# Both products of a transformer MLP by seven products of halves, in two phases, on one Trainium2 core

## The reference, cut to what matters

```python
def sqrelu_mlp(xn, w1, w2):                   # xn (1024, 1024), w1 (1024, 4096), w2 (4096, 1024)
    return jnp.square(jax.nn.relu(xn @ w1)) @ w2

    f = sqrelu_mlp(rms_norm(h, g[2]), ffn_w1[i], ffn_w2[i])
    h = h + rms_norm(f, g[3])
```

## Time and profile before

| | |
|---|---|
| median of 3 runs | 2694.79 us (2693.78 to 2695.09) |
| the profiled execution's own time | 2696.62 us |
| its span, first to last instruction | 2694.4 us |
| mean granted TensorE clock | 0.977 |
| PE busy | 2523.3 us (94%), 12064 matmuls |
| DVE busy | 1754.1 us (65%) |
| POOL busy | 1235.9 us (46%) |
| ACT busy | 1037.8 us (39%) |
| MLP of layer 0, first projection to the end of `down_last` | from 955.9 us |
| MLP of layer 1, the same | from 2006.3 us |

### The profile page before, as it was taken

The page is one execution under the profiler, slowest core; times in us unless marked ns, Lnnn a source line. Parts: engine busy times, 40 slices in busy tenths (PEclk is TensorE's granted clock), DMA queues, the critical chain, the costliest instruction groups (busy, mean ns, idle before and its releaser), DMA issues.

```text
span 2694.4 us, 35810 instructions
## 1 busy us (share of the span) xinstructions
PE 2523.3 (94%) x12064; PEld 2078.4 (77%) x12064; DVE 1754.1 (65%) x3033; ACT 1037.8 (39%) x1849; POOL 1235.9 (46%) x661
## 2 busy tenths in 40 slices
PE   7899999798898999999999999977899999999998
PEld 6689877676676878888888887856777888888886
DVE  5599999766665566676566746175565765665565
ACT  5543533556555251223232235265543222223222
POOL 2112776544544123565566422366622465565541
PEclk9999989899999999999999999999999999999999
DMA  4471733533444621111221134654452121101213
GB/s 145 68 111 27 165 98 115 190 98 91 140 131 131 239 97 55 55 32 45 62 62 54 39 110 128 156 150 122 125 173 103 31 63 54 54 27 51 70 39 125
DMA packets 260043, 258.15 MB, mean 96 GB/s; under 512 B 11906, under 2 KB 219810, under 8 KB 257620
## 3 DMA queue, kind: packets, MB, share of 16 engines
q1 hardware_dynamic: 250436, 239.22, 31.6%
q10 hardware_dynamic: 9216, 16.78, 2.1%
q0 software_dynamic: 272, 0.62, 0.1%
HBM read 181.60 MB, written 74.97 MB: 95 GB/s over the span
## 4 chain that ended last, share of the span: by engine, by line
PE 78%; POOL 7%; DVE 6%; issue 4%; ACT 3%; DMA 1%; SPq 0%; DVEq 0%; POOLq 0%; ACTq 0%
PE ps L446 75%; POOL attn_out_split L1071 1%; POOL attn_out L1069 1%; PE ps L2318 1%; DVE probs_T L1930 1%; POOL w_split L398 1%; DVE logits L1895 1%; PE ps L564 1%; ACT relu_scores L1285 1%; DVE masks L1799 1%; POOL attn_out_split L1067 1%; DVE acc L1657 1%; POOL attn_out_low L1064 1%; ACT probs_T L1436 1%; DVE acc L1646 1%
## 5 line engine op out<-in xcount | busy, mean ns | idle before, releaser
L446 PE MATMUL ps<-xn_T,w_split 128*128 128x512 f32 x4608 | 1058.9, 391 | 1.6 <-DVE xn_T L1734 1.5
L446 PEld LDWEIGHTS ps<-xn_T,w_split 128*128 128x128 f32 x4608 | 867.6, 189 | 186.4 <-issue 3.0
L398 POOL TENSOR_TENSOR w_split<-w_raw,w_split 128x1024 fp32r<-128x1024 f32 x92 | 225.9, 2465 | 638.0 <-ACT w_split L391 637.7
L446 PE MATMUL ps<-w_comb,hid_comb 128*128 128x512 f32 x2016 | 458.9, 389 | 0.0
L446 PEld LDWEIGHTS ps<-w_comb,hid_comb 128*128 128x128 f32 x2016 | 378.4, 188 | 78.6
L2093 DVE TENSOR_TENSOR acc<-acc,ps 128x512 f32<-128x512 f32 x480 | 303.0, 683 | 77.7 <-PE ps L446 72.6
L446 PE MATMUL ps<-w_split,hidden 128*128 128x512 f32 x1344 | 310.8, 392 | 8.9 <-POOL w_split L398 6.3
L446 PEld LDWEIGHTS ps<-w_split,hidden 128*128 128x128 f32 x1344 | 253.5, 189 | 63.2 <-issue 6.6
L2073 DVE TENSOR_TENSOR hid_blocks<-hid_blocks 128x512 f32<-128x512 f32 x96 | 85.5, 891 | 263.9 <-ACT hid_blocks L1538 263.1
L594 POOL TENSOR_TENSOR w_split<-w_raw,w_split 128x1024 fp32r<-128x1024 f32 x52 | 132.8, 2555 | 247.7 <-ACT w_split L589 247.7
L1533 ACT ACTIVATE hid_comb<-hid_blocks 128x512 fp32r<-128x512 f32 (+1 forms) x120 | 95.2, 802 | 216.7 <-PE ps L446 84.4
(11 more groups left out here) (206 smaller groups left out, 3477.3 us busy)
## 6 DMA issues: line engine op xcount, KB each, us to landing
w_raw<-in_w SPq DMA_DIRECT2D x104, 512.0 KB, 4.2
q_scratch<-q_split SPq DMA_DIRECT2D x128, 128.0 KB, 2.5
q_tile<-q_scratch ACTq DMA_DIRECT2D x64, 256.0 KB, 2.7
cat_scratch<-attn_out_split SPq DMA_DIRECT2D x128, 128.0 KB, 2.6
w_raw<-in_w_in SPq DMA_DIRECT2D x30, 512.0 KB, 4.7
unit_tile<-cat_scratch SPq DMA_DIRECT2D x48, 256.0 KB, 3.6
h_scratch<-acc SPq DMA_DIRECT2D x24, 512.0 KB, 4.1
w_raw_rest<-in_w SPq DMA_DIRECT2D x24, 512.0 KB, 6.5
```

Source lines behind the costliest of these rows:

```text
L398: nc.gpsimd.tensor_tensor(whl[:, n0 % 4, 1, :], wraw[:, n0 % 4, :], whl[:, n0 % 4, 0, :].bitcast(F32), ALU.subtract).then_inc(w_lo, 1)
L446: return nc.tensor.matmul(out_ap, stat, mov, start=start, stop=stop)
```

## The change

In each layer the first 4 inner tiles are still computed directly by `project_first`. The other 28 go through "up" in seven products too, and the whole of "down" follows after the whole of "up":

- **Input sums.** The up product needs four sums of quarters of the input (`x_sums`). POOL forms three raw quarters (high plus low, `raw`: 6 operations of 128x1024, four of them while the normalisation still runs, two after the second transposes). DVE forms the fourth and the four sums (10 operations of 128x1024), and their low parts (8 of 128x1024); ACT their high parts.
- **First rows.** ACT does ReLU and square of the first 4 tiles. DVE brings them into the form of seven operands (8 sums of 128x512) between the input sums, before it takes out the first up product. Each layer then stores 14 such blocks (3.5 MB) to DRAM.
- **Up.** 7 iterations (LOOPS = 6 and one more) of two column pairs, 7 products each, a product is 12 matmuls into one PSUM bank: 14 x 12 = 168 matmuls an iteration. POOL: per pair 4 sums of w1 blocks and 7 low parts, all 128x512. DVE: per pair 8 operations from PSUM, 4 squares and 4 sums in SBUF, all 128x512. SP loads the next two w1 tiles and stores the pair's 7 blocks to a DRAM scratch (`h_operand_scratch`).
- **Down.** 28 products (4 groups of 7; the last group is half as deep). Per product: a load of its inner operand from the scratch (1 MB), high parts by ACT, low parts by DVE for the inner operand (`h_low`, 128x2048) and by POOL for w2 (`down_low`, 128x2048; 4 sums of the same size per group), 48 matmuls, takes by DVE as before. Then `change_quarters` once, and `down_last` for inner tiles 28 to 31.
- `sp_gains` of the MLP's end moves behind the up phase; `CREDIT` and the old rings go.

```diff
+        def half_pair(p, i):                      # POOL, per pair
+            k = 7 * p
+            a11, a12, a21, a22 = [w1_block(p, c, h) for c in range(2) for h in range(2)]
+            s2 = w1_operand(L, k + 2)
+            pool.wait_ge(w1_ld[p], loads + 32 + 32 * i)
+            nc.gpsimd.tensor_tensor(a21, a11, a21, ALU.subtract).then_inc(w1_sum, 1)
+            up_low(k, i)
+            up_low(k + 1, i)
+            pool.wait_ge(a_full, w1_slot_free(L, k + 2) + 14 * i)
+            up_sum(p, 1, i, s2, a22, a21, ALU.subtract)
+            up_sum(p, 2, i, a12, s2, a12, ALU.subtract)
+            nc.gpsimd.tensor_tensor(a11, s2, a11, ALU.add).then_inc(w1_sum, 1)
+            up_low(k + 2, i)
+            up_low(k + 3, i)
...
+        split_lo(pool, L["tf"] + LOOK)            # POOL, ahead of the loop
+        pool.wait_ge(a_full, first_pos(sn, 0, 0) + 1)
+        pool.wait_ge(a_free, trans_pos(sn, 0, KT - 1) + 1)
+        raw(0, 0, 0)
+        raw(1, 0, 4)
+        pool.wait_ge(a_free, trans_pos(sn, 1, KT - 1) + 1)
+        raw(3, 1, 4)
+        head(0)
+        with pool.Fori(0, LOOPS, 1) as i:
+            rest(i)
+            head(i + 1)
+        rest(LOOPS)
+        for g in range(4):                        # POOL, down
+            b11, b12, b21, b22 = [w_block(g, k)[:] for k in range(4)]
+            z = 7 * g
+            down_low(z)
+            pool.wait_ge(w2_ld[1], w_loads(lay, g))
+            pool.wait_ge(w2_ld[3], w_loads(lay, g))
+            down_sum(g, 0, b12, b22, b12, ALU.subtract)
+            down_sum(g, 1, b11, b12, b11, ALU.add)
+            down_low(z + 1)
+            down_low(z + 2)
+            down_sum(g, 2, b21, b11, b21, ALU.subtract)
+            down_low(z + 3)
+            down_sum(g, 3, b22, b22, b11, ALU.subtract)
+            for r in range(4, 7):
+                down_low(z + r)
...
         for j in range(4):                        # ACT
-            relu_square(first_pos(sn, j, 0), L["f0"] + j, j, 0)
-            square_hid(L["f0"] + j, j, 0)
+            relu(j, 0)
...
+        act.wait_ge(h_st, 128 * sn)
+        relu(0, 1)
+        relu(1, 1)
+        up_high(0, 0)
+        up_high(1, 0)
+        x_sum_high(6, 0)
+        x_sum_high(4, 2)
+        relu(2, 1)
+        x_sum_high(9, 3)
+        x_sum_high(11, 1)
+        up_high(2, 0)
+        up_high(3, 0)
+        relu(3, 1)
...
         xn_low(sn, 1, 0, KT)                      # DVE, ahead of the loop
+        for k in range(2):
+            js = slice(2 * k, 2 * k + 2)
+            raw12 = first_op(nc.vector.tensor_tensor(xsum[:, 2, js, :], xt[:, 1, 0, js, :].bitcast(F32), xt[:, 1, 1, js, :].bitcast(F32), ALU.add))
+        t3 = x_sum_op(2, 3, 2, ALU.subtract, raw12)
+        t2 = x_sum_op(0, 2, 0, ALU.add, t3)
+        squared(5)
+        first_sum(d[:, 0, :], e[:, 0, :], d[:, 0, :], ALU.subtract)
+        x_sum_op(3, 3, 0, ALU.subtract, t2)
+        x_sum_op(1, 0, 1, ALU.subtract, t2)
+        squared(6)
+        n1 = first_sum(d[:, 1, :], e[:, 1, :], d[:, 1, :], ALU.subtract)
+        x_sum_low(7, 0)
+        x_sum_low(9, 2)
+        squared(11)
+        n2 = first_sum(d[:, 4, :], d[:, 2, :], d[:, 0, :], ALU.subtract, n1)
+        first_sum(d[:, 5, :], d[:, 4, :], e[:, 0, :], ALU.add, n2)
+        first_sum(d[:, 6, :], d[:, 4, :], e[:, 2, :], ALU.subtract, n2)
+        x_sum_low(12, 3)
+        x_sum_low(14, 1)
+        squared(16)
+        n3 = first_sum(d[:, 7, :], d[:, 3, :], d[:, 1, :], ALU.subtract)
+        first_sum(h_more[:, 0, :], d[:, 7, :], e[:, 1, :], ALU.add, n3)
+        first_sum(h_more[:, 1, :], d[:, 7, :], e[:, 3, :], ALU.subtract, n3)
...
+        for z in range(len(PRODUCTS)):            # DVE, down
+            for q in range(4):
+                take(z, q)
+                if q == 1 and z + 2 < len(PRODUCTS):
+                    h_low(z + 2)
...
+        def up_product(k, i, bank0):              # PE, up
+            p, o = divmod(k, 7)
+            pe.wait_ge(w1_lo, 98 * lay + k + 1 + 14 * i)
+            if o in (2, 3, 5, 6):
+                pe.wait_ge(x_lo, 8 * lay + {2: 2, 3: 4, 5: 6, 6: 8}[o])
+            pe.wait_ge(a_free, up_group(L, k) - 3 + 14 * i)
...
+            for kt in range(4):
+                cols = slice(kt * P, (kt + 1) * P)
+                mm(bank, wh[:, cols], xh[:, kt, :], kt == 0, False)
+                mm(bank, wh[:, cols], xl[:, kt, :], False, False)
+                last = mm(bank, wl[:, cols], xh[:, kt, :], False, kt == 3)
+            last.then_inc(a_full, 1)
...
+        def load_h(z):                            # SP, down
+            g, r = PRODUCTS[z]
+            products_done(sp, L, z - 3)
+            n = pairs_of(g)
+            sp.dma_start(h_split(z, 1, raw=True), hopd[lay, 4 * g:4 * g + n, H_BLOCK[r]].rearrange("k r t -> r k t")).then_inc(h2_ld[z % 3], 16)
...
+        load_w(0, 0)                              # SP, from up to down
+        sp.wait_ge(a_full, up_group(L, 14 * LOOPS + 9))
+        for p in range(2):
+            sp.wait_ge(h_sp[p], h_stores(lay, p, 32))
+        load_h(0)
+        sp.wait_ge(w1_lo, lows + 98)
+        load_w(0, 1)
+        load_w(0, 3)
+        sp.wait_ge(a_full, up_group(L, 14 * LOOPS + 10))
+        load_w(0, 2)
+        sp.wait_ge(a_full, up_group(L, 14 * LOOPS + 12))
+        sp.wait_ge(h_sp[0], h_stores(lay, 0, 208))
+        load_h(1)
+        load_h(2)
```

More of the change, by code:

```diff
@@ new lines, in head, with rest, down_low @@
+        def head(i):
+            half_pair(0, i)
+        def rest(i):
+            for k in range(4, 7):
+                up_low(k, i)
+            half_pair(1, i)
+            for k in range(11, 14):
+                up_low(k, i)
+        def down_low(z):
+            g, r = PRODUCTS[z]
+            pool.wait_ge(w2_hi, w_high_count(lay, z))
+            nc.gpsimd.tensor_tensor(w_split2(z, 1), w_operand2(z), w_split2(z, 0).bitcast(F32),
+                                    ALU.subtract).then_inc(w2_lo, 1)
@@ L1127, in pool_ffn @@
+        for n in range(L["tf"] + 4, L["tf"] + 8):
             split_lo(pool, n)
@@ new lines, in act_ffn, with relu, x_sum_high @@
+        sums, splits, loads = 62 * lay + 6, 98 * lay, 224 * lay
+        def relu(j, th):
+            f = first_pos(sn, j, th)
+            act.wait_ge(a_full, f + 1)
+            dst = (last_rows if th else first_rows)[:, j, :]
+            nc.scalar.activation(dst, ps[:, f % 4, :], ACT.Relu).then_inc(a_free, 1)
+            act.wait_ge(a_free, f + 1)
+            nc.scalar.activation(dst, dst, ACT.Square).then_inc(x_hi, 1)
+        def x_sum_high(count, k):
+            act.wait_ge(h0_ok, 18 * lay + count)
+            for e in range(2):
+                nc.scalar.activation(xsum_hi[k][:, 2 * e:2 * e + 2, :], xsum[:, k, 2 * e:2 * e + 2, :], ACT.Copy).then_inc(x_hi, 1)
@@ new lines, in dve_ffn, with first_op, squared, first_sum @@
+        lay = L["lay"]
+        oks = 104 * lay
+        done = [18 * lay]
+        def first_op(ins):
+            done[0] += 1
+            ins.then_inc(h0_ok, 1)
+            return done[0]
+        def squared(count):
+            dve.wait_ge(x_hi, 16 * lay + count)
+        def first_sum(dst, x, y, op, count=None):
+            if count:
+                dve.wait_ge(h0_ok, count)
+            return first_op(nc.vector.tensor_tensor(dst, x, y, op))
+        def x_sum_op(dst, x, y, op, count=None):
+            dve.wait_ge(w1_sum, 62 * lay + 6)
+            if count:
+                dve.wait_ge(h0_ok, count)
+            for e in range(2):
+                js = slice(2 * e, 2 * e + 2)
+                last = first_op(nc.vector.tensor_tensor(xsum[:, dst, js, :], xsum[:, x, js, :], xsum[:, y, js, :], op))
+            return last
@@ new lines, in dve_ffn @@
+        with dve.Fori(0, LOOPS // 2, 1) as i2:
+            for e_ in range(2):
+                for p in range(2):
+                    pair(p, i2 * 2 + e_, bank0 + 14 * e_)
+        for p in range(2):
+            pair(p, LOOPS, bank0 + 14 * LOOPS, last=True)
+        h_low(1)
+        for z in range(len(PRODUCTS)):
+            for q in range(4):
+                take(z, q)
+                if q == 1 and z + 2 < len(PRODUCTS):
+                    h_low(z + 2)
+        dve.wait_ge(b_free, L["bf"] + 112)
@@ L2505, in pe_ffn @@
-        pe.wait_ge(f_lo, CREDIT + L["f0"] + 12)
-        down_last(pe, L["tn"] - 4, L["stage"] + 1,
-                  lambda part: pe.wait_ge(f_lo, CREDIT + L["f0"] + 16))
+        bank0 = up_group(L, 0)
+        with pe.Fori(0, LOOPS // 2, 1) as i2:
+            for e in range(2):
+                for k in range(14):
+                    up_product(k, i2 * 2 + e, bank0 + 14 * e)
+        for k in range(14):
+            up_product(k, LOOPS, bank0 + 14 * LOOPS)
+        for z in range(len(PRODUCTS)):
+            down_product(z)
@@ L2509, in program @@
+        pe.wait_ge(w2_lo, w_low_count(lay, 13) + 4)
+        down_last(pe, L["tn"] - 4, L["stage"] + 1, lambda part: None)
     with nc.Block() as block:
```

694 lines of the change are left out of this document (346 added, 348 removed).

## The result

The changed kernel takes 2713.91 us (median of 4 runs, 2710.11 to 2718.11) where the kernel before takes 2694.28 (2693.09 to 2695.09): a ratio of 1.0073, 95% interval 1.0060 to 1.0086, so slower by 0.7%. The forecast was 2712. Its profiled execution took 2714.72 us with a span of 2712.9.

The account below looks back on a forecast made before the run. TensorE, busy for 94% of the span, was taken to bound the kernel. Losses of 52.1 us a layer, twice 104.2, less 87.1 for matmuls saved, gave +17.1: 2712 us against the median 2694.79, range 2652 to 2750.

Parts of the forecast that it names:

- The matmuls: MLP of both layers: 384 fewer matmuls at 0.2267 us each, 87.1 us less if PE stays fed.
- End of the normalisation: Before the second projection: POOL's raw operations take turns with DVE's sums and scalings, net +6.6 us a layer, bounds 0 and 8.4.
- Input sums and first rows: Start of up: DVE's 26 operations alternate with POOL's, so the first take is late, +20 us a layer, bounds 0 and 22.
- T: Time when the eight low parts before the second projection end; the first take was put at 50 to 51 us later.
- Rival A: Faster: POOL and DVE don't meet at a layer's start, so the first two losses go; 2659 us, chance 0.27.
- Steady up phase: Up pairs after the start: POOL and DVE need 16.7 of 19.0 us of ports, so no loss, 0.
- B: Rival, slower still: the up phase binds, 1.4 us a pair, 2751 us, chance 0.10.
- my slack of 1.0 us: Steady up: DVE's critical stretch was to end 1.0 us before the fifth product wants that bank.
- From up to down: Start of down: products 0 and 1 wait for low parts by POOL and DVE, +14.1 us a layer, bounds 5 and 20.
- U: End of the up phase; product 0 was to start 6.8 us later, product 1 to be ready 25 us later.
- Rest of down: Later down groups: third group's second product 3.9 us late, last group loses 1.5; +5.4 a layer, bounds 0 and 15.
- Clock: After PE stalls the clock is slow: two unhidden stalls a layer at 3.0 us each, +6.0 a layer, bounds 2 and 10.

Follow-up runs that it names:

- E4: The changed kernel with POOL's first four input sums moved behind the second transposes; one run of 2709.72 us.
- E1: The changed kernel with one more wait: POOL rests early in each layer's up phase until DVE has done its 18 counted steps; 2693.40 us, ratio 0.9986 of the kernel before.
- E8: The changed kernel with two more unused DVE operations of 128x512, two SBUF operands each, per pair of the up phase; one run of 2776.18 us.
- E2: The changed kernel with POOL's second low part ahead of the second sum in each down group; 2703.52 us, ratio 1.0028 of the kernel before.
- E9: The changed kernel with POOL's four low parts of the last tiles spread over products 10 to 13; 2705.58 us, ratio 1.0037 of the kernel before.
- E6: The changed kernel with the edits of E1 and E2, and ACT making w2's high part first for product 0; 2679.47 us, ratio 0.9947 of the kernel before.

## Why the prediction was right

**The matmuls** (-43.5 a layer): 11680, and an iteration of 168 in 38.08 us is 0.2267 each. Right.

**End of the normalisation** (+6.6, measured +5.2 and +5.4). From the first projection to the second: before 32.05 us (955.88 to 987.93), after 37.25. The cause was the stated one (E4 gives back the 0.90 us of before). The rows came 8.2 us later (8.4 worked out), but the transposes and their low parts then took 6.1 us instead of my 7.3.

**Input sums and first rows** (+20.0, measured +18.7 and +17.6): 16.28 + 2.00 + 0.41 us of waits in layer 0. T was 997.9 and the take came at T + 49.6, against my T + 50 to 51. The sign that I gave was a wait near 20 us and `x_sums` operations of 2 to 3.4 us; they show 16.28 and 1.7 to 2.3, so the place and the cause were right and each operation was held for a little less. POOL did the 20 operations that I had counted, but rested 7.9 us for ACT among them where I had put 2. Rival A fell with these rows: 1.2 us is what it asked for, and E1, which takes only POOL's presence away, shows 1.16.

**Steady up phase** (0): right, pairs of 19.04 us, so B fell. But my slack of 1.0 us was in truth 0.35 in every second pair and 1.7 in the others, since POOL has a rest in one of them. E8 shows how near B was: a turn costs 1.6 us there, more than the slack of every second pair.

**From up to down** (+14.1, measured 13.9 in both layers): product 0 at U + 6.6 (6.8), product 1 at U + 24.7 (25), that is 6.59 and 7.26 us. Of the second, only 4.20 us show as a wait, where my sign said 5 to 8, since product 0 ran 3.1 us longer at the slow clock. That clock cost nothing there, as product 1 waited for POOL anyway, and I hadn't foreseen it. Nor had I foreseen that this start has two forms, by which engine goes first. My working had the load land at U - 4, which lies between the two: 3.4 to 3.9 us before U gives the 6.6 of the forecast, 4.6 to 5.2 gives 10.8 (E2). That the kernel after shows the first form in both layers was luck.

**Rest of down** (+5.4, measured 5.7 and 6.7): the place was right, the size was made of two errors. The second product of the third group was late by 5.7 to 6.7 us, not 3.9. POOL's four low parts took 11.56 us and not 9.6, since DVE's turns among them weren't counted: that is the difference in layer 0, and 2 of the 2.8 us in layer 1. The 1.5 us of the last group didn't come.

**Clock** (+6.0, measured 7.1 in layer 0). Granted clock (third from the end) in the 3 to 4 us behind the waits of 4.20, 16.28 and 5.74 us: 0.50 in each, that is 1.2 GHz; the stretch behind that of 6.59 shows 0.50 too.

```profile
1330.90:1334.90 4.00, 3.98 (x9) 3.13 (x10) 0.00 (x0) 3.08 (x2) 4.00 (x1) 0.50 1.05 394
...
1048.20:1051.20 3.00, 3.00 (x7) 2.42 (x8) 2.81 (x4) 0.00 (x0) 1.70 (x2) 0.50 0.95 352
1491.50:1495.50 4.00, 3.96 (x9) 3.14 (x10) 0.00 (x0) 2.98 (x2) 4.00 (x1) 0.50 0.02 4
```

Four stalls a layer, not two, but at 2.1 to 2.6 us each where they cost anything (12 matmuls in 4.84 us instead of 2.72; 672 in 154.88 instead of 152.3; 288 in 67.76 instead of 65.3), and 3.1 at product 0 that was hidden. So the term was wrong in its parts, too few stalls at too high a price each, and came out near by luck.

Together the losses of layer 0 are 5.2 + 18.7 + 13.9 + 5.7 + 7.1 = 50.6 against my 52.1, and 50.6 - 43.5 = 7.1 against 7.5 us of the stage. For both layers the stage gives +16.3 where I had +17.1; the other 2.2 us of the 18.5 between the spans are the stretches outside. That the total met the measurement to 2 us is better than its terms deserve: several were off by 1 to 2 us, in both directions.

What stays open: why the load of the inner operand lands up to 1.7 us earlier in some layers, with which the order of DVE and POOL at the start of the down phase changes; the 4.4 us by which E1's ratios exceed its waits; and 2 of the 4.9 us left in layer 1 of E9.

## What to carry to other kernels

When a change gives two engines that take turns more work, don't add up busy times. Count, ahead of each thing that the critical engine waits for, the instructions of both engines that fall into that stretch; each can cost a full instruction of the other, and costs nothing extra where the other rests (the even pairs of E8). The remedy is order: have the engine that isn't needed rest or work elsewhere (a single wait gave back 0.9%), and keep pieces of its work away from the dense stretches. And a stall moved is not a stall removed: E4 and E6 took one away and met all or part of it again at a later one. Nor is an earlier input always a gain: in layer 0 of E2, where the load landed earlier, POOL went first, and PE started 4.2 us later.
